# Turning the expert tiles on VectorE in 32x32 blocks instead of on TensorE, one-hots of four tokens at once, and an RMS-norm factor made per token

## The reference

```python
q = (xb @ w_q).reshape(T, 8, 2, 128)                      # 8 heads, two halves
s = einsum('thjd,hjkd->thjk', q, sub_keys)                # 128 keys a half
sv, si = top_k(s, 16)                                     # then the best 16 of 16 x 16 sums
eidx = i1 * 128 + i2                                      # expert number, 16384 experts
g = softmax(cs)                                           # weights of the 16 chosen
act = gelu(einsum('td,thkd->thk', xb, expert_u[eidx]))
out = einsum('thk,thkd->td', g * act, expert_v[eidx])

rmsnorm(x, g) = x * rsqrt(mean(x * x) + EPS) * g
```

## Time and profile before

| what | value |
|---|---|
| median of 3 runs | 5176.4 us (5175.56 to 5180.27) |
| the profiled execution, its own time | 5174.52 us |
| span of its trace | 5172.8 us |
| mean granted TensorE clock | 0.947 |
| busy: TensorE, VectorE, ScalarE, GpSimd | 4694.7, 2315.6, 1422.0, 352.1 us |

### The profile page before, as it was taken

The page is one execution under the profiler, slowest core; times in us unless marked ns, Lnnn a source line. Parts: engine busy times, 40 slices in busy tenths (PEclk is TensorE's granted clock), DMA queues, the critical chain, the costliest instruction groups (busy, mean ns, idle before and its releaser), DMA issues. The chain is left out here.

```text
span 5172.8 us, 60896 instructions
## 1 busy us (share of the span) xinstructions
PE 4694.7 (91%) x23260; PEld 3920.4 (76%) x23260; DVE 2315.6 (45%) x3698; ACT 1422.0 (27%) x1441; POOL 352.1 (7%) x213
## 2 busy tenths in 40 slices
PE   8998998999996889968887899799999899999997
PEld 6886667877876668857776687688887777888886
DVE  4323234324324543225666243465655654355554
ACT  2213433223221332223332222232222222222221
POOL 0000000000000000001112000000000000233331
PEclk9998999999997789979998999899999999999998
DMA  3232012232231022211111232223333433555553
GB/s 106 95 100 66 33 33 84 92 92 89 90 93 37 0 82 97 89 43 58 49 49 33 73 89 93 66 98 123 125 122 127 158 142 151 197 193 191 191 193 114
DMA packets 446289, 511.43 MB, mean 99 GB/s; under 512 B 22105, under 2 KB 394965, under 8 KB 445157
## 3 DMA queue, kind: packets, MB, share of 16 engines
q1 hardware_dynamic: 446180, 510.01, 29.5%
HBM read 440.74 MB, written 69.21 MB: 99 GB/s over the span
## 5 line engine op out<-in xcount | busy, mean ns | idle before, releaser
L78 DVE TENSOR_TENSOR w_lo<-w_raw,w_hi 128x2048 fp32r<-128x2048 f32 (+2 forms) x322 | 676.2, 2102 | 1292.5 <-ACT w_hi L72 1292.5
L72 ACT CAST w_hi<-w_raw 128x2048 fp32r<-128x2048 f32 (+2 forms) x322 | 555.7, 1730 | 1128.5 <-PE psum L2738 491.6
L94 PE MATMUL psum<-h_hi_ffn,w_hi 128*128 128x512 f32 x1280 | 497.9, 389 | 0.0
L95 PE MATMUL psum<-h_lo_ffn,w_hi 128*128 128x512 f32 x1280 | 497.9, 389 | 0.0
L96 PE MATMUL psum<-h_hi_ffn,w_lo 128*128 128x512 f32 x1280 | 497.9, 389 | 0.0
L94 PE MATMUL psum<-h_hi_peer,w_hi 128*128 128x512 f32 x1120 | 444.8, 397 | 3.1 <-DVE w_lo L78 1.9
L96 PE MATMUL psum<-h_hi_peer,w_lo 128*128 128x512 f32 x1120 | 436.9, 390 | 0.0
L95 PE MATMUL psum<-h_lo_peer,w_hi 128*128 128x512 f32 x1120 | 436.2, 389 | 0.0
L2736 PE MATMUL psum<-pr_act_hi,w_hi 128*128 128x512 f32 x1024 | 398.3, 389 | 0.0
L2737 PE MATMUL psum<-pr_act_lo,w_hi 128*128 128x512 f32 x1024 | 398.3, 389 | 0.0
L2738 PE MATMUL psum<-pr_act_hi,w_lo 128*128 128x512 f32 x1024 | 398.3, 389 | 0.0
(11 more groups left out here) (441 smaller groups left out, 8332.9 us busy)
## 6 DMA issues: line engine op xcount, KB each, us to landing
w_raw<-in_ffn_w_gate_up_dram SPq DMA_DIRECT2D x176, 512.0 KB, 4.2
w_raw<-in_peer_u_dram SPq DMA_DIRECT2D x128, 512.0 KB, 4.1
w_raw<-in_peer_v_dram SPq DMA_DIRECT2D x128, 512.0 KB, 4.2
w_raw<-in_w_in_dram SPq DMA_DIRECT2D x64, 512.0 KB, 4.5
peer_hidden<-pr_q SPq DMA_DIRECT2D x64, 512.0 KB, 2.6
peer_gates<-pr_staged SPq DMA_DIRECT2D x8, 4096.0 KB, 12.7
pr_back<-peer_hidden SPq DMA_DIRECT2D x64, 512.0 KB, 6.1
pr_gate<-peer_gates SPq DMA_DIRECT2D x64, 512.0 KB, 7.1
```

Source lines behind the costliest of these rows:

```text
L72: c.nc.scalar.copy(c.hi[:, slot, :cols], c.raw[:, slot, :cols]).then_inc(c.hi_ready, 1)
L78: c.nc.vector.tensor_tensor(c.lo[:, slot, :cols], c.raw[:, slot, :cols], c.hi[:, slot, :cols].bitcast(F32), ALU.subtract).then_inc(c.lo_re ...
L94: c.nc.tensor.matmul(out, w_hi, x_hi, start=(n == 0), stop=False)
L95: c.nc.tensor.matmul(out, w_hi, x_lo, start=False, stop=False)
```

## The change

- A unit's tile is loaded in four transfers, each for 32 partitions: partition b*32+e gets, of eight rows of experts, the 256 features of band b. VectorE then turns it in place in 32x32 blocks, two instructions of 128x1024 (`turn`, now on VectorE). After it partition p holds the features 8p to 8p+7, for which elements are read eight apart (`u_view`). ScalarE and VectorE read `raw` instead of PSUM for the high and the low part, in two instructions for the high and two for the low part.
- The tokens need the same order. Their split parts are stored to DRAM during the queries (`store_h`, 4 MB) and read back in the new order, chunk by chunk, while TensorE finishes the last query tile (`reload_h`), whose products now run chunk by chunk for both outputs.
- TensorE no longer turns. The products of the units alternate between PSUM banks 0 to 1 and 2 to 3, so Gelu has a unit's time to take them.
- VectorE's queue: in each unit first the turn of the next tile, which waits until the tile two before it is used, then the routing piece or the quads "before", then the subtraction, then the quads "between". `EARLY` is 10, with two pieces in a row after the split of tile 5.
- Quads: 28 units with 4 or 5 each instead of 24 with 5 or 6. The unweighted one-hots of a quad are built by one instruction of 128x512.
- Norms of width 512: the sums are made with the tokens on partitions, 128x4, the factor is made there, spread over a diagonal (128x512) and brought to all partitions with a matrix of ones; scaling reads it from PSUM.

```diff
         dve.wait_ge(self.summed, run + 1)
-        nc.vector.tensor_scalar(rstd[:, :].rearrange("p (b n) -> p b n", b=len(self.banks)), self.ps,
-                                1.0 / D, EPS, ALU.mult, ALU.add).then_inc(self.steps, 1)
-        dve.wait_ge(self.rooted, run + 1)
-        nc.vector.reciprocal(rstd[:, :], rstd[:, :]).then_inc(self.steps, 1)
-        dve.wait_ge(self.steps, run * self.STEPS + self.STEPS)
+        if self.by_token:
+            nc.vector.tensor_scalar(self.col[:, :], self.ps[:, 0, 0:TC], 1.0 / D, EPS, ALU.mult, ALU.add
+                                    ).then_inc(self.steps, 1)
+            dve.wait_ge(self.rooted, run + 1)
+            nc.vector.reciprocal(self.col[:, :], self.col[:, :]).then_inc(self.steps, 1)
+            dve.wait_ge(self.steps, run * self.STEPS + self.STEPS)
+            tokens = [P, TC, P]
+            nc.vector.tensor_tensor(rstd[:, :].rearrange("p (t k) -> p t k", t=TC),
+                                    self.c.ident[:, :].unsqueeze(1).broadcast_to(tokens),
+                                    self.col[:, :].unsqueeze(2).broadcast_to(tokens), ALU.mult
+                                    ).then_inc(self.spread, 1)
+            dve.wait_ge(self.widened, run + 1)
...
-            mm = self.c.nc.tensor.matmul(self.ps[:, b, :], self.c.ones[:, :], self.sq[:, 0, lo:hi], start=True,
-                                         stop=True)
-        mm.then_inc(self.summed, 1)
+        mm = self.c.nc.tensor.matmul
+        if self.by_token:
+            for t in range(TC):
+                ins = mm(self.ps[:, 0, t:t + 1], self.sq[:, 0, t * P:(t + 1) * P], self.c.ones[:, 0:1], start=True,
+                         stop=True)
+            ins.then_inc(self.summed, 1)
+            pe.wait_ge(self.spread, self.run + 1)
+            mm(self.ps[:, 0, :], self.c.ones[:, :], self.rstd[:, :], start=True, stop=True).then_inc(self.widened, 1)
...
+def u_view(c, slot, a):
+
+    return c.raw[:, slot, a * D:(a + 1) * D].rearrange("p (q d k) -> p k q d", q=P // BAND, d=BAND)
+
+
 UNITS = KEYS // 2
+ROWS_LOADED = 16
+BAND = 32
+U_MORE = 32 * (UNITS // 2)
 PIECES = 5
-EARLY = 8
+EARLY = 10
 CHOSEN_AT = (NH * PIECES - EARLY)
 SPREAD_AT = CHOSEN_AT + 2
-SPREAD_ROUNDS, ROUND_UNITS = 4, 6
+SPREAD_ROUNDS, ROUND_UNITS = 2, 14
 SPREAD_END = SPREAD_AT + SPREAD_ROUNDS * ROUND_UNITS
 QUAD = 4
 RING = 4
 GROUP_QUADS = TG // QUAD
-ROUND_QUADS = 2 * GROUP_QUADS
-QUADS = ((2, 3), (2, 3), (3, 3), (2, 3), (2, 3), (3, 3))
+ROUND_GROUPS = 4
+ROUND_QUADS = ROUND_GROUPS * GROUP_QUADS
+QUADS = ((2, 2), (2, 3)) * 6 + ((2, 3), (2, 3))
...
             def u_tile(use, j, n):
-                load_tile(c, sp, use, j, u_parts(c, j, u, n * 2))
+
+                sp.wait_ge(c.begun, 1)
+                sp.wait_ge(c.lo_ready, 2 * use + j + 1)
+                rows = u.rearrange("(q e) d -> e q d", e=BAND)
+                for b in range(P // BAND):
+                    dst = c.raw[b * BAND:(b + 1) * BAND, j, :].rearrange("p (q n) -> p q n", n=BAND * KD)
+                    src = rows[:, bass.ds(n * 8, 8), b * BAND * KD:(b + 1) * BAND * KD]
+                    sp.dma_start(dst, src).then_inc(c.tile_loaded[j], 16)
+
+            def store_h():
+
+                sp.wait_ge(pre.lo_done, (pre.run + 1) * KD)
+                for m in range(2):
+                    sp.dma_start(h_rows[m].rearrange("(k p) t -> p k t", p=P), h[m][:, :, :].bitcast(F32)
+                                 ).then_inc(h_stored, 16)
+
+            def reload_h():
+
+                sp.wait_ge(h_stored, ROWS_LOADED + 32)
+                for k in range(KD):
+                    sp.wait_ge(h_free, k + 1)
+                    for m in range(2):
+                        sp.dma_start(h[m][:, k, :].bitcast(F32), h_rows[m].rearrange("(p k) t -> p k t", p=P)[:, k, :]
+                                     ).then_inc(h_back[k // 4], 16)
...
+            for i in range(1, NH // 2):
                 for j in range(2):
                     load_tile(c, sp, u0 + i, j, wide_parts(c, j, w_q, (i * 2 + j) * 256))
                     keys_of(i, j)
-            for n in range(3):
-                u_tile(uA + n // 2, n % 2, n)
+                if i == 1:
+                    store_h()
+            u_tile(uA, 0, 0)
+            u_tile(uA, 1, 1)
+            reload_h()
+            u_tile(uA + 1, 0, 2)
...
+            def copy_hi(j):
+
+                for a in range(2):
+                    hi = c.hi[:, j, a * D:(a + 1) * D].rearrange("p (k q e) -> p k q e", k=KD, q=P // BAND)
+                    ins = nc.scalar.copy(hi, u_view(c, j, a))
+                ins.then_inc(c.hi_ready, 1)
+
             def turned_hi(n):
-                use, j = uA + n // 2, n % 2
                 act.wait_ge(turned, n + 1)
-                act.wait_ge(c.tile_used, 2 * use + j + 1)
-                nc.scalar.copy(c.hi[:, j, :], turn_ps).then_inc(c.hi_ready, 1)
+                copy_hi(n % 2)
...
-                nc.scalar.activation(q[:, n % 2], ps[:, 4:6, :], ACT.Gelu).then_inc(gelued, 1)
+                at = 2 * (n % 2)
+                nc.scalar.activation(q[:, n % 2], ps[:, at:at + 2, :], ACT.Gelu).then_inc(gelued, 1)
...
             turned_hi(0)
+            weigh(1)
...
+            def turn(n):
+
+                j = n % 2
+                dve.wait_ge(c.tile_loaded[j], 32 * uA + 64 * (n // 2) + 64)
+                dve.wait_ge(c.tile_used, 2 * uA + n + 1)
+                for a in range(2):
+                    part = u_view(c, j, a)
+                    ins = V.transpose(part, part)
+                ins.then_inc(turned, 1)
+
             def turned_lo(n):
+
                 j = n % 2
                 dve.wait_ge(c.hi_ready, 2 * uA + n + 1)
-                V.tensor_tensor(c.lo[:, j, :], turn_ps, c.hi[:, j, :].bitcast(F32), ALU.subtract
-                                ).then_inc(c.lo_ready, 1)
+                for a in range(2):
+                    lo, hi = (t[:, j, a * D:(a + 1) * D].rearrange("p (k q e) -> p k q e", k=KD, q=P // BAND)
+                              for t in (c.lo, c.hi))
+                    ins = V.tensor_tensor(lo, u_view(c, j, a), hi.bitcast(F32), ALU.subtract)
+                ins.then_inc(c.lo_ready, 1)
...
+                    wide = [P, QUAD, KEYS]
+                    toks = slice(at * QUAD, (at + 1) * QUAD)
+                    V.tensor_tensor(second[:, k % RING], c.iota[:, :].unsqueeze(1).broadcast_to(wide),
+                                    chosen[:, 1, toks].unsqueeze(2).broadcast_to(wide), ALU.is_equal)
                     for t in range(QUAD):
                         tok = at * QUAD + t
-                        V.tensor_scalar(second[:, k % RING, t, :], c.iota[:, :], chosen[:, 1, tok:tok + 1], None,
-                                        ALU.is_equal)
                         ins = V.tensor_scalar(first[:, k % RING, t, :], c.iota[:, :], chosen[:, 0, tok:tok + 1],
...
-                piece(n - 2)
-            for p in range(NH - 2, EARLY):
+                piece(n - 2 if n < 6 else n - 1)
+                if n == 5:
+                    piece(n - 1)
+            for p in range(NH - 1, EARLY - 2):
                 piece(p)
+            turn(0)
+            piece(EARLY - 2)
+            turned_lo(0)
+            piece(EARLY - 1)
             for n in range(CHOSEN_AT):
-                turned_lo(n)
+                turn(n + 1)
                 piece(EARLY + n)
-            turned_lo(CHOSEN_AT)
+                turned_lo(n + 1)
+            turn(CHOSEN_AT + 1)
             finish(NH - 1)
             turned_lo(CHOSEN_AT + 1)
+            turn(SPREAD_AT)
             turned_lo(SPREAD_AT)
             dve.wait_ge(chosen_taken, 3)
             for o in range(SPREAD_ROUNDS):
                 for x in range(ROUND_UNITS):
                     before, between = quads_of(x)
+                    n = SPREAD_AT + o * ROUND_UNITS + x + 1
+                    turn(n)
                     build(o, before)
-                    turned_lo(SPREAD_AT + o * ROUND_UNITS + x + 1)
+                    turned_lo(n)
                     build(o, between)
             for n in range(SPREAD_END + 1, UNITS):
+                turn(n)
                 turned_lo(n)
...
+                if last:
+                    jobs = wide_jobs(c, h, j)
+                    for k in range(KD):
+                        for out, pair, _ in jobs:
+                            (w_hi, w_lo), (x_hi, x_lo) = pair(k)
+                            nc.tensor.matmul(out, w_hi, x_hi, start=k == 0, stop=False)
+                            nc.tensor.matmul(out, w_hi, x_lo, start=False, stop=False)
+                            mm = nc.tensor.matmul(out, w_lo, x_hi, start=False, stop=k == KD - 1)
+                        mm.then_inc(h_free, 1)
...
-            def turn(use, j):
-
-                pe.wait_ge(c.tile_loaded[j], 32 * use + 32)
-                pe.wait_ge(c.lo_ready, 2 * use + j + 2)
-                part = raw_tile(c, j, 2, D)
-                for a in range(2):
```

(35 more changed lines are left out.)

111 lines of the change are left out of this document (63 added, 48 removed).

## The result

The changed kernel takes 5321.69 us (median; 5321.11 to 5346.4) against 5175.98 us before: ratio 1.0295, 95% interval [1.0266, 1.0325]. I had forecast 5203 with a range of 5155 to 5365, slower with a chance of 0.67. So the sign and the range held, and the likeliest case did not: the time lies between it and two of the rivals, the loads (5345) and "far steps cost" (5362), and the profile has to say which.

What follows compares the result with a forecast made beforehand. Phase A was taken as bound by TensorE, with 122 us of turns removed but VectorE's queue order then making TensorE wait. 5176.4 + 37.4 (phase A) - 11 (norms) = 5203 us, range 5155 to 5365.

Steps and rivals of the forecast that it cites:

- the likeliest case: Main case for the whole kernel: 5203 us, own range 5185 to 5225, chance 0.47.
- the loads: Rival: a tile's four loads run one after another, 16.4 us against 11.6, +140, giving 5345; chance 0.06.
- far steps cost: Rival: 32-byte steps make turn and subtraction on VectorE 4.5 us each, giving 5362; chance 0.19.
- the price of a turn and of the split subtraction: VectorE, per unit: 1.22 us per 128x1024 transpose, 2.36 for a turn; the split subtraction 2.36 as well.
- +37.4: Phase A, the experts' hidden values: ends at 4477.0 instead of 4439.6 us.
- The order decides: VectorE's queue: work behind each waiting turn delays TensorE, which stands 4.4 us at the start of each one-hot unit.
- The clock: TensorE, one-hot units: half clock up to 8.4 us after the stand, 1.3 us in each of 28 units, 36 us.
- The rival in which the clock holds by itself: No half clock in one-hot units: 36 us go, 5166; chance 0.28 together with the cheap-turn rival.
- End of the queries: TensorE stands 8.8 us before the last query tile; with 2.1 lost to half clock, +10.9.
- Norms: Eight norms of width 512: 1.4 us less each, -11 us in all, bounds 0 and -28.
- One-hots of four tokens: VectorE, phase A: one 128x512 comparison makes a quad 1.63 us instead of 1.81; a one-hot unit takes 21.56.
- Loads: Four transfers per tile on 32 partitions, 4.1 us each, cost nothing up to 11.6 us between release and turn.

Runs made afterwards that it cites:

- experiment 1: Changed kernel with the 32 elements of a block next to each other (4 bytes apart instead of 32), tokens brought back to match: 5199.18 us, ratio 1.0031.
- experiments 3: Changed kernel, 32-byte steps kept, with the first four one-hot quads built ahead of the turn and ScalarE staging two ahead of its copy: 5224.12 us, ratio 1.0095.
- experiment 8: Changed kernel with near steps, four quads built ahead of the turn, and routing pieces 5 and 6 behind the last query tile's split: 5020.34 us, ratio 0.9685.
- experiment 4: Experiment 1 with 17 TensorE products that nobody reads at the start of each one-hot unit: 5164.81 us, ratio 0.9975.
- experiment 6: Kernel before the change with only the new norm put in: 5168.05 us, ratio 0.9977.
- experiment 7: Kernel before the change with only one 128x512 comparison for four tokens in place of four of 128x128: 5161.54 us, ratio 0.9973.
- experiment 5: Changed kernel with routing pieces 5 and 6 moved behind the split of the last query tile: 5324.97 us, ratio 1.0297.
- experiment 9: Experiment 8 with ten products that nobody reads ahead of each wait for the normed weights in the window attention: 4996.01 us, ratio 0.9655.

## Why the prediction was wrong in its likeliest case and right around it

**The step that failed** is the price of a turn and of the split subtraction: "I take 1.22, the usual price at this size". Both bounds were there (0.69 and 2.29), and I chose by the size of the instruction and not by how far its elements lie apart. The rival "far steps cost" had the mechanism, with a chance of 0.19, and experiment 1 shows it: with the distance alone changed, 2.09 becomes 1.22 and the profiled run falls from 5346.4 to 5199.2, 4 us from the forecast of 5203. Of the 171.9 us between the two traces, 147 are this one term; the other 25 are what I had forecast as +37.4 and -11. The median of after is nearer, 5321.7, only because most of its runs fall in the shorter group. The forecast had no term for the stage that makes that difference, so this part of the nearness is luck; the longer group, 5346, lies in the range as well.

**What misled me** was the row that I set against the rival: ScalarE's copy out of PSUM at 512-byte steps, which shows no price. It read another memory. For SBUF, no row that I had read spoke, and the price taken should have stayed open. The Trainium skill ("SBUF — State Buffer", Door 1) was no witness against itself either: what it says of PSUM's 8-byte lines is that they slow TensorE's products, not copies.

**The rival's own sizes.** It had two steps per column, 4.5 us for turn and for subtraction. Measured: 3.93 to 4.25 and 4.07. It kept ScalarE's copy at its old price, but that reads the far elements too: in the one-hot unit it is 4.08 us, and the subtraction waits 0.95 for it. Five units took 71.5 us (gap to gap, 3646.67 to 3718.16) against the rival's 73.3, a one-hot unit 23.49 against 23.9. That and the shorter norm gain make 5346 of 5362, and the other group of runs is 25 us below that.

**The order decides**: held. The chain of handoff, turn, one-hots was forecast at 4.4 and is 4.13 with near steps, 5.67 with far ones. Removing it (experiments 3 and 8) is worth 122 us with far steps; with near steps and the query end, 179.

**The clock**: held in what it costs. 36 us forecast for all 28 units, 34.4 measured (experiment 4). I had half clock from the first product on in every unit, which is so in 28 of 28 after and in 23 of 28 in experiment 1. The rival in which the clock holds by itself fell: the windows after and in experiment 1 show 0.88 and 0.89.

**End of the queries**: held. 8.8 forecast, 8.52 there; 10.9 for the whole, 9.5 measured by its removal.

**Norms**: -11 forecast, -7 measured, inside the bounds of 0 and -28. The bound of -28 was no mere margin: in 2 of 10 runs the kernel gained 32, and their mean granted clock is 0.951 against 0.946 in the others. No trace of these two shows the stage; in the kernels whose traces do, it is the window attention.

**One-hots of four tokens**: as an edit of its own it is worth 14 us. In my sum it was hidden in the unit of 21.56, where it makes the chain 0.2 shorter per quad.

**Loads**: "cost nothing" held. No wait of TensorE and no turn on VectorE is for a load, and a transfer of 256 KB lands 4.6 us (median) after its issue, the four of a tile issued within 1.9 us, which rules out the rival of 16.4 us.

**What the order of the changes hid.** Compared with before, 122 us of turns were taken off TensorE, and the kernel became 146 us slower. Experiment 8 shows that the 122 were there to be had: with the same turns on VectorE, phase V starts at 4288 instead of 4440, 152 us earlier. Of these, 7 are the norms' (experiment 6) and 122 the turns'. TensorE's waits for one-hots from 3380 us on fall from 49.9 to 2.9 us, 47 more, of which the four-token comparison alone brings 13 (experiment 7). Against them stand 28.3 us of waits for the low part of a tile, 4.3 before. That is 152.

## What to carry to other kernels

Ask of every operand of an added instruction how far its neighbouring elements lie apart, not only how many there are; if no row reads that memory at that distance, leave the price open. When work moves to an engine that has time to spare, write down its queue in order for one unit: a step that must wait for the end of a unit must not stand ahead of what the next unit starts with. And a short stand of TensorE costs its length and then some at half clock, so a gap of 4.1 us was worth some 5.4 here (experiment 4).

## What the runs showed of the hardware that I had not expected

The price of distance in SBUF is a step: 1.22 us for a transpose of 128x1024 with elements 4 or 8 bytes apart, 2.03 at 16, 2.09 at 32; nothing between 8 and 16 was tried. The step of 32 bytes raises ScalarE's copy from 1.05 to 2.14 as well, so it is not a matter of one engine.

A wait and a slow clock can go together for a whole stage, and with the wait filled neither was seen. TensorE at two steps of the window attention after, and in the run of experiment 5:

```profile
1706.28 1.92 PE L1340 MATMUL psum<-ident,sw_s 128*128 128x128 f32 x8 [2.39 <-DVE sw_s L1274]
1723.53 1.97 PE L1340 MATMUL psum<-ident,sw_s 128*128 128x128 f32 x8 [2.47 <-DVE sw_s L1274]
```

```profile
1715.13 2.70 PE L1352 MATMUL psum<-sw_probs_t,sw_v 128*64 128x128 f32 x14 [1.54 <-ACT sw_probs_t L1225]
1728.02 1.74 PE L1352 MATMUL psum<-sw_probs_t,sw_v 128*64 128x128 f32 x14 [1.54 <-ACT sw_probs_t L1225]
1731.03 1.09 PE L1340 MATMUL psum<-ident,sw_s 128*128 128x128 f32 x8 [0.69 <-DVE sw_s L1274]
```

One has steps of 17.2 us, a wait of 2.4 ahead of the turned weights (L1340) in each, and a clock of 0.71 over the stretch. The other has steps of 12.4 to 12.9, the same wait at 0.7 and one of 1.54 ahead of the next products (L1352), and 0.91. From the first to the last of the 128 products of L1340 it is 124.7 us in the one and 98.1 in the other, which is the difference of some 25 us between the groups. The kernel before shows 0.72 there in its trace, and its 45 runs beside these experiments all lie between 5173.7 and 5178.8 us; with the shorter norm ahead of the stage, a run falls in either. With ten small products ahead of the wait (experiment 9) all four runs are in the shorter group, where one of four was without them (experiment 8). That the slow clock lengthens the wait and the wait keeps the clock low fits this, but is argued and not shown; what decides at the entry of the stage wasn't tried.
